# Where a stage computes its input norm among its first tiles, and where an activation table is loaded, in a two-model fp32 kernel

## The reference, cut to what matters

```python
def rms_norm(x, w):
    xf = x.astype(jnp.float32)
    y = xf * lax.rsqrt(jnp.mean(xf * xf, axis=-1, keepdims=True) + EPS)
    return (y * w.astype(jnp.float32)).astype(x.dtype)

def swiglu(x, w_gu, w_down):
    gate, up = jnp.split(x @ w_gu, 2, axis=-1)
    return (jax.nn.silu(gate) * up) @ w_down
...
# first block, each of 2 layers
h = h + 0.5 * swiglu(rms_norm(h, ffn1_norm[l]), ffn1_w_gu[l], ffn1_w_down[l])
...   # mixer: latent attention and a gated recurrence
h = h + 0.5 * swiglu(rms_norm(h, ffn2_norm[l]), ffn2_w_gu[l], ffn2_w_down[l])
...
# second block: macaron_ffn norms the input and the branch's output
h = swiglu_2(rms_norm_2(x, pre_g), w_gate, w_up, w_down)
return x + MACARON_WEIGHT * rms_norm_2(h, post_g)
```

## Time and profile before

| | |
|---|---|
| median of 3 runs | 2541.1 us (2532.03 to 2544.89) |
| the profiled execution | 2539.87 us, of which the span of the trace is 2537.8 us |
| PE busy | 2381.6 us, 94% of the span |
| DVE, ACT, POOL busy | 57%, 47%, 24% |
| mean granted TensorE clock | 0.954 of full |

### The profile page before, as it was taken

How to read it: one execution, slowest core, us unless ns; L and a number is a source line. 1 busy time by engine, 2 the same in 40 slices (tenths; PEclk the granted TensorE clock), 3 DMA queues, 4 the chain that set the end, 5 groups by cost and what they waited for, 6 DMA issues and landing times.

```text
span 2537.8 us, 50443 instructions
## 1 busy us (share of the span) xinstructions
PE 2381.6 (94%) x18338; PEld 2302.7 (91%) x18338; DVE 1443.6 (57%) x1950; ACT 1187.5 (47%) x1749; POOL 614.6 (24%) x617
## 2 busy tenths in 40 slices
PE   7999989899999999899999999986999999987998
PEld 7999886799999999886899999986999999977998
DVE  5556774455545557853655555466654655465553
ACT  5445543344445436432354355456654445445553
POOL 4321130043213211310332132123431122111320
PEclk9999998899999999987999999998999999988999
DMA  6554332145545544331355545533555465532553
GB/s 206 176 184 156 112 117 73 64 159 183 184 155 169 187 155 136 100 100 34 117 177 184 167 144 190 194 113 108 160 192 195 146 203 185 187 116 77 181 199 108
DMA packets 99268, 380.29 MB, mean 150 GB/s; under 512 B 10911, under 2 KB 13087, under 8 KB 99144
## 3 DMA queue, kind: packets, MB, share of 16 engines
q1 hardware_dynamic: 99144, 378.63, 45.9%
HBM read 377.52 MB, written 3.16 MB: 150 GB/s over the span
## 4 chain that ended last, share of the span: by engine, by line
PE 63%; issue 26%; POOL 4%; DVE 2%; POOLq 2%; ACT 1%; DVEq 1%; DMA 0%; ACTq 0%; SPq 0%
PE bank L527 20%; PE bank L529 20%; PE bank L528 20%; POOL kd L1921 2%; POOLq L1872 1%; POOL midlo L1929 1%; PE bank L588 1%; PE bank L589 1%; PE bank L590 1%; PE bank L545 0%; POOLq L1860 0%; DVE h L1617 0%; POOL reclo L1924 0%; DVE xlo L1322 0%; POOL acc L1862 0%
## 5 line engine op out<-in xcount | busy, mean ns | idle before, releaser
L1311 DVE TENSOR_TENSOR wlo<-raw,whi 128x1024 fp32r<-128x1024 f32 (+1 forms) x660 | 892.2, 1362 | 549.2 <-ACT whi L925 548.9
L527 PE MATMUL bank<-xhi,wlo 128*128 128x272 f32 (+1 forms) x3392 | 983.8, 290 | 2.7 <-DVE wlo L1311 2.0
L529 PE MATMUL bank<-xhi,whi 128*128 128x272 f32 (+1 forms) x3392 | 978.8, 289 | 0.0
L528 PE MATMUL bank<-xlo,whi 128*128 128x272 f32 (+1 forms) x3392 | 976.4, 288 | 0.0
L925 ACT ACTIVATE whi<-raw 128x1024 fp32r<-128x1024 f32 (+1 forms) x660 | 728.8, 1117 | 448.8 <-PE bank L529 418.2
L527 PEld LDWEIGHTS bank<-xhi,wlo 128*128 128x128 f32 x3392 | 650.2, 192 | 3.8 <-DVE wlo L1311 2.4
L529 PEld LDWEIGHTS bank<-xhi,whi 128*128 128x128 f32 x3392 | 649.3, 191 | 0.0
L528 PEld LDWEIGHTS bank<-xlo,whi 128*128 128x128 f32 x3392 | 648.7, 191 | 0.0
L527 PE MATMUL bank<-hidhi,wlo 128*128 128x272 f32 (+1 forms) x1408 | 400.9, 285 | 0.0
L529 PE MATMUL bank<-hidhi,whi 128*128 128x272 f32 (+1 forms) x1408 | 399.8, 284 | 0.0
L528 PE MATMUL bank<-hidlo,whi 128*128 128x272 f32 (+1 forms) x1408 | 399.7, 284 | 0.0
(11 more groups left out here) (313 smaller groups left out, 2763.2 us busy)
## 6 DMA issues: line engine op xcount, KB each, us to landing
raw<-ffn_gu SPq DMA_DIRECT2D x352, 512.0 KB, 3.5
raw<-ffn_down SPq DMA_DIRECT2D x128, 704.0 KB, 4.1
raw<-mix SPq DMA_DIRECT2D x120, 512.0 KB, 3.5
raw<-rec SPq DMA_DIRECT2D x28, 512.0 KB, 3.6
raw<-kv SPq DMA_DIRECT2D x16, 512.0 KB, 4.2
raw<-att SPq DMA_DIRECT2D x16, 512.0 KB, 3.7
bias_rows<-rows SPq DMA_DIRECT2D x8, 256.0 KB, 4.3
bias<-bias_rows SPq DMA_DIRECT2D x1, 1536.0 KB, 10.0
```

The source lines that it names most:

```text
L527: pe.matmul(out, wlo[:, slot, w], xh(i), start=(i == 0), stop=False)
L528: pe.matmul(out, whi[:, slot, w], xl(i), start=False, stop=False)
L529: mm = pe.matmul(out, whi[:, slot, w], xh(i), start=False, stop=(i == last))
L1311: dve.tensor_tensor(wlo[:, k, 0:cols], raw[:, k, 0:cols], whi[:, k, 0:cols].bitcast(F32), ALU.subtract).then_inc(lo_made, 1)
```

## The change

Three edits.

1. In `stage_tiles` and in `ffn` on PE, `norm_sum` is called behind tile 4 instead of tile 3, and `norm_back` behind tile 5 instead of tile 4. "The fifth" and "the sixth" tile count from one.
2. In `first_splits` on ACT, `norm_std` stands behind the fourth split instead of ahead of it; on DVE the same for `norm_inv`.
3. In the attention on ACT, `warm_sqrt()` is called ahead of the output projection's tiles.

```diff
@@ stage_tiles, PE
                     k8_tile(q + t // RING, t % RING, j + t - 3 if t >= 7 else None, early_bank(t), src, c)
-                    if t == 3:
+                    if t == 4:
                         input_norm(x, n, c)()
-                    if t == 4:
+                    if t == 5:
                         norm_back(n, c)
@@ ffn, PE
-                    if t == 3 and main_norm:
+                    if t == 4 and main_norm:
                         input_norm(x, n, c)()
-                    if t == 4 and main_norm:
+                    if t == 5 and main_norm:
                         norm_back(n, c)
@@ first_splits, ACT
                 for k in range(RING):
-                    if k == 3 and main_norm:
-                        norm_std(n, c)
                     split_hi(q + 1, k, CH8, j + k + 1)
                 if main_norm:
+                    norm_std(n, c)
                     norm_copy(n, c)
@@ attention, ACT
+                warm_sqrt()
                 for m in range(KD):
                     act.wait_ge(tile_done, j + 8 + m + 1)
@@ first_splits, DVE
                 for k in range(RING):
-                    if k == 3 and main_norm:
-                        norm_inv(n, c)
                     split_lo(q + 1, k, CH8)
                 if main_norm:
+                    norm_inv(n, c)
                     dve.wait_ge(rstd_made, rstd_copies(n))
```

## The result

The changed kernel takes 2550.6 us (median of 6 runs, 2543.2 to 2554.6); the kernel before, run beside it, takes 2541.2 (6 runs, 2529.6 to 2544.9). The ratio is 1.0055, 95% interval 1.0033 to 1.0077: slower by 0.33 to 0.77%, some 14 us by the ratio. The medians alone differ by 9.4 us (0.37%); 12.5 were forecast. Ratios leave out two executions of the kernel before, at 2636.7 and 12715.9 us, that ran far slower than all others. The profiled execution took 2547.4 us with a span of 2545.4, 7.6 more than before's 2537.8.

A forecast was written before the change was run, and what follows sets the result against it. PE, busy 94% of the span, bounds the kernel. Stage terms sum to +3.6 us and clock falls add +8.9; +12.5 on the profiled 2539.87 us gives 2552.4, in median terms 2553 us, range 2543 to 2562.

The forecast's parts named there:

- the clock did not stay up: Rival at tile 8: the standstills come but PE's clock stays up, about 2545 us; chance 0.20.
- the chain did not fit: Rival: the work behind the broadcast fits before tile 8, layers cost nothing, 2528 to 2529 us; chance 0.05.
- spreading rival: Splits behind tile 8 lag too, each stage loses another tile: 20 us more, 2570; chance 0.05.
- Layers: Four layer feed-forwards: no wait to win, PE stands 2.12 us at tile 8 in each, +8.5 us.
- F4, F5: Feed-forwards: F4's tile 8 comes 2.3 us later; F5's 1.0 us later in spite of its removed 1.35 us wait.
- F7: Feed-forward: 0.4 us of the sum's 3.24 us wait stays, broadcast 1.49 us earlier, tile 8 earlier: -2.0 us.
- REC: Stage with convolutions: broadcast comes 1.49 us earlier and tiles 7 and 8 hang on it: -1.5 us.
- KV: KV stage: broadcast keeps its time, two tiles fewer stand between it and tile 8: -2.3 us.
- tile 4 covers 1.36: KV's sum: moving it behind tile 4 hides its whole 1.36 us wait for POOL's `acc`.
- ATT: Attention stage: tile 4 covers the sum's 1.43 us wait and most reaches the scores: -1.4 us (-0.6 to -1.6).
- Edit 3: Attention's branch norm: early table load cuts PE's idle time at the broadcast from 1.53 to 0.55 us: -1.0 us.
- The clock: Behind seven new standstills at tile 8, six falls of PE's clock at 1.49 us each: +8.9 us (0 to 10.4).

The follow-up runs named there:

- the second run of the changed kernel: The changed kernel measured again without any edit, beside the kernel before: 2548.0 us against 2537.3, ratio 1.0040.
- the second experiment: Kernel before with sum and broadcast moved only in REC, KV, ATT and F7, plus the attention's early root table: 2533.4 us against 2535.4, ratio 0.9990.
- the filled kernel: Changed kernel with 18 extra, unused matmuls on PE ahead of tile 8 in seven feed-forwards: 2539.3 us against 2535.4 of the kernel before, ratio 1.0013.
- the kernel with the early root alone: Kernel before with only `warm_sqrt()` moved ahead of the attention's output projection: 2536.4 us against 2538.4, ratio 0.9987.
- the kernel with the layers alone: Kernel before with sum and broadcast moved only in the four layer feed-forwards, no early root: 2548.6 us against 2535.4, ratio 1.0049.

## Why the prediction was right

**The outcome.** 2550.6 us stands 2.4 below the forecast of 2553 and inside 2543 to 2562. The ratio says slower by 0.55%, just over the line at 0.5%; that it fell on this side is luck, as the chances of 0.47 and 0.48 said, and the second run of the changed kernel, at 0.40%, fell on the other. The forecast's mechanism came, and its rivals didn't: the clock did not stay up (five of seven fell), the chain did not fit, no second tile waits in a feed-forward, the table load cost nothing. How near the sum came owes something to luck too: the terms below are off by up to 0.9 us each, and the errors cancel. (The spreading rival's 2570 is itself some 3 us low: 2553 + 20 = 2573.)

**Layers, 2.12 each.** Right in kind, 0.2 too small each. The broadcast to tile 8 took 44.35 - 34.61 = 9.74 us before and 9.06 after; a tile later makes 9.06 + 3.02 - 9.74 = 2.34 us. The slack of 0.90 was taken from the split's end to tile 8's start, but behind a stop PE starts tile 8 only some 0.2 us after the split's end (45.90 against 44.47 + 1.23 = 45.70 on DVE), which a running PE doesn't pay.

**F4, F5.** The same: F4 has (1512.04 - 1503.47) + 2.84 - (1500.10 - 1491.16) = 2.47 against 2.33, with 1503.47 and 1491.16 the two broadcasts; F5 has (1834.69 - 1826.15) + 2.84 - (1821.84 - 1812.90) - 1.35 = 1.1 against 1.0. F5's stretch in the table, +2.8, is this and a fall of 1.6.

**F7.** From the first tile of the stage to tile 8 it took 2362.22 - 2332.09 = 30.13 us before and 2369.64 - 2341.56 = 28.08 after: -2.05 against -2.0. The wait of 3.24 left 0.45, as said. The forecast gave it one of the seven chances of a fall, and its clock stayed up.

**REC.** Sum to tile 8: 1702.72 - 1685.79 = 16.93 before, 15.36 after: -1.57 against -1.5. The idle time moved rather than went: 0.45 at the sum, then 3.54 and 0.44 in the place of 0.70 and 2.01.

**KV.** -2.9 against -2.3. The step that failed is "tile 4 covers 1.36": 0.56 us of waiting stayed. PE's tiles up to the sum ran faster than before: with the fifth tile the forecast's way leads to 2006.88 - 1991.21 - 1.36 + 2.84 = 17.15 us from the stage's first tile, and PE was there after 2022.12 - 2005.65 - 0.56 = 15.91. `acc` was 0.80 us later than before (16.47 against 15.67), since POOL's two additions took 4.45 us where they had taken 3.65. So the sum stands 0.7 us earlier than forecast in spite of the wait, which is the 0.6 that KV won beyond the forecast. The wait of 1.36 in the earlier trace rows was a draw, as the second experiment shows for F5.

**ATT.** Mis-sized. -1.4 was taken from bounds of -0.6 and -1.6, and from the first tile to the scores the rows give (2277.17 - 2249.59) - (2266.33 - 2238.06) = 27.58 - 28.27 = -0.7. The scores' wait for the last eviction grew from 0.52 to 1.00, since DVE, started later by the broadcast, runs its evictions and splits there without a gap and no longer follows PE; and the tiles up to the sum took 17.01 us where 15.29 - 1.43 + 2.84 = 16.70 were due. The term that was too large is "most comes through": of 1.4, 0.5 went into that wait and 0.3 into slower tiles. The row that showed a wait already there pointed to the lower bound.

**Edit 3.** 1.5 against 1.0. The term left out that the broadcast itself, whose row is 1.22 us long behind the wait of 1.53, becomes 0.71.

**The clock.** Six falls x 1.49 = 8.9 against five x 1.6 = 8.0. Number and price were each off by a little and in opposite ways. That a like row stood in REC made this term; the filled kernel, 3.3 us slower than before (interval 0.3 to 6.6) where the sum without the clock says 3.6, shows that it was the clock. Which of the seven fall is a draw, as the second run of the changed kernel shows.

**Together**: 9.4 + 2.5 + 1.1 - 2.05 - 1.6 - 2.9 - 0.7 - 1.5 = +4.2 without the clock (forecast +3.6), and +8.0 for it: 12.2 against 12.5. The stages' 10.4 in the table is less, above all by 1.4 in the first layer's second feed-forward, where a slow stretch of the kernel before, at 741.64, has no counterpart after.

## What to carry to other kernels

When a small step (a norm's sum and broadcast) moves later in the queue of the engine that bounds the kernel, first measure the chain that hangs on it and ends at that same engine: here 9.06 us from broadcast to the tile that needs its split. Before, three tiles and the broadcast itself covered it (9.74 us); after, two are left (6.7). A wait removed at the step can turn into a loss if the chain is longer than what is left between (F5: 1.35 us of waiting removed, and tile 8 came 1.1 us later); take work off the chain that doesn't need the step (here a split, 12.7 us in place of a loss), and price each new standstill with what it does to the clock, which here was 1.6 us on top of 2.2, in five cases of seven.

## What the runs showed of the hardware

- **A fall of the clock isn't certain at 2.2 us.** In both profiles of the changed kernel five of seven stretches fell behind waits of 2.15 to 2.31 us; in the first, 779.36 (2.15) and 2369.64 (2.27) stayed at full clock, 2.4 GHz, and in the second the first feed-forward (2.17) and F7 (2.28). The same instruction behind the same wait thus fell in one execution and not in the other. None fell behind 0.64 to 0.89 us, and none behind a wait filled with matmuls. One fall costs some 1.6 us; the 0.63 to 0.66 of these stretches is a mean over time at 1.2 and time at 2.4 GHz.
- **Useless work can pay.** 18 matmuls of 128 columns (2.12 us), put where PE would have stood still, made the kernel faster by 5.5 to 10.7 us without starting tile 8 earlier in its stage.
- **A wait in one profile may be one of two values.** F5's sum waited 1.35 us in one profile and 3.25 in another with the same instructions in its stage, and POOL's two additions ahead of it took 3.64 and 4.71 us; KV's sum waited 1.36 us before and 3.50 in the kernel with the early root alone, and ATT's 1.43 before and 3.27 in the kernel with the layers alone; one kernel's own runs spread over some 15 us (2529.6 to 2544.9). Gains counted from waits at sums carry this uncertainty, the length of a chain doesn't: 9.03 to 9.06 us from broadcast to tile 8 in the layers, in the profiles of four kernels.
